# Order of 512-wide and 256-wide products within a weight block, on one core

## Chip, core and metric

The kernel runs on one NeuronCore of a Trainium2 chip. What is compared is the device time of one execution in microseconds (us). It is one program in fp32, with matrix products fed in fp32r (a rounded form of fp32 that TensorE takes in one pass).

## What is computed

Two transformer-like blocks, one after the other, on 256 tokens of width 2048. The first is an RG-LRU mixer with a gated side input, the second a conformer and HGRN mixer followed by a squared-ReLU MLP. Cut to what matters here:

```python
# first block
proj = rmsnorm(x) @ a_w_in                  # stages xb, gate
y = (lru_scan(conv(xb)) * silu(gate)) @ a_w_out          # gates, aout
h = x + rmsnorm(y); h = h + sigmoid(h @ ple_w_gate) * (p @ ple_w_proj)   # pleg, plep
# second block, with modulation vectors from silu(c) @ w_mod
u = modulate(rmsnorm(h)); uc = modulate(rmsnorm(ctx))
i, ff, fb, q, g, cv, cg, gc, gh = split(u @ w_in)        # i, ff, fb also of uc
y_h = readout(hgrn_bidir(q, i, ff, fb, state(uc)), g) @ hgrn_out_w       # hout
y_c = conformer(cv, cg) @ conv_pw_w                      # pw
y = (sigmoid(gc) * y_c + sigmoid(gh) * y_h) @ w_out      # wout
x = h + ga * rmsnorm(y)
out = x + gf * rmsnorm(square(relu(modulate(rmsnorm(x)) @ mlp_w1)) @ mlp_w2)   # mlp1, mlp2
```

All activations stand transposed: features on the 128 partitions, the 256 tokens along the free axis. A tile of a result is 128 features by 256 tokens, summed over the 128-row slices (kt) of its input features.

## The kernel before

**Products in parts.** To keep more bits than fp32r has, both sides are split into a high part and the remainder, the low part. A weight block of 128 x 1024 (eight 128 x 128 weight tiles) lands by DMA in WF (7 buffers); ScalarE (ACT) copies it to WH (the high part, 4 buffers), VectorE (DVE) subtracts to get WL (the low part, 4 buffers). The moving operand lies in SR with its high and low parts side by side, 256 columns each. A full product is WH by high, WH by low and WL by high; low by low is left out.

**Wide and narrow products.** In the stages listed in HALVES (line 54: pleg, cv, cg, q, hout, gh, wout, mlp1, mlp2, pw, gc), one weight tile takes two products: a *wide* one of 512 columns (WH against high and low parts side by side, into the whole PSUM bank) and a *narrow* one of 256 columns (WL against the high part, added to the bank's second half). ACT and DVE add the bank's two halves when the tile is done. The other stages differ: xb, gate, aout, g and a few others use three 256-wide products per weight tile; ff and fb use three 512-wide ones (two token sets at once, read through a strided pattern); i uses three 512-wide ones with the weights as the moving operand. Tile 15 of pleg and of wout (WHOLE, line 55) is done like xb.

**Order.** `timetable()` writes out by hand one list of steps that all engines walk through, each doing its own. A step `prod` is one weight tile (kt) of one result tile. `linear` (line 359) makes one result tile from two weight blocks of eight kt each (h = 0 and 1; for pw and hout from one block), through `product` (line 336), which also calls `tick` after each kt. Every `stride` ticks (4 from the stage cv on, so every four kt), `tick` adds one step of the background work: convolution, states, the HGRN scan (7 levels for each of 4 head pairs, each with a group of TensorE products between ACT and DVE work) and its readout. `linear_quad` (line 370) makes four result tiles at once in four banks, at the start of the stages xb, pleg, cv, i and mlp1, while ACT and DVE are still making the moving operand, two kt per block; its steps `make` do that. Weight blocks are prepared three blocks ahead (LA).

**On TensorE.** The function `product` in `tensor_program` (line 868) turns a step into instructions. It waits on `w_lo` (WL of the block is there, and so WH) at the block's first product, on `free[g]` for the bank at a tile's first one, and on a stage's counter for each kt of its moving operand: `n_lo` (normed input, cv to mlp1), `ys2_lo` (wout), `mid_lo` (mlp2), `ds_lo` (pleg). A wait that was already passed is not issued again. The last product of a block adds to `prod`, which frees WH and WL of that block and tells of finished tiles. For a HALVES stage the two products of a weight tile are ordered by kt: wide then narrow at even kt, narrow then wide at odd kt, so that in a tile made alone pairs of equal width meet.

```python
                for low in ((False, True), (True, False))[kt % 2]:
                    if low:
                        last = mm(cross((kind, j)), wl, hi, False, stop)
                    else:
                        last = mm(bank_of((kind, j))[:, :], wh, flat(moving[kind][:, kt, :, :]), start, stop)
```

Of the kernel before, what the change touches and what calls it, by code (L numbers as in the profile page):

```python
# [74 lines left out]
def timetable():  # L75
# [254 lines left out]
    def tick(n=1):  # L330
        st["since"] += n
        if st["since"] >= st["stride"]:
            st["since"] = 0
            step()

    def product(what, n, first=True, last=True):

        at = len(steps)
        for k in range(n):
            kind, j, h = what  # L340
            off = k * 512 + j % 4 * P if kind == "plep" else (j[2] * 2 + k) * T + j[3] * P if kind == "gates" else k * P
            steps.append(("prod", (kind, j), 8 * h + k, off, first and k == 0, last and k == n - 1, k == n - 1,
                          st["used"], "both"))
            if k + 1 < n:
                tick()
        st["prod"] += 1
        return at

# [21 lines left out]
    def linear_quad(kind, js):  # L370
        for j in js:
            new_tile((kind, j))
        made = 0

        def make(until):
            nonlocal made
            while kind != "i" and made < min(until, KT):
                steps.append(("make", kind, made))
                made += 1

        if kind == "xb":
            make(2)
            prepare(ahead=0)
            low_parts()
        for b in range(8):

            make(2 * b + (4 if kind in ("xb", "pleg") else 2))
            begin(min(LA, b + 1) if kind == "xb" else LA)
            make(2 * b + 4)
            if kind == "xb":  # L390
                if b == 0:
                    steps.append(("load_xr",))
                if b < 6:
                    steps.append(("small", b + 1))
                if b in (5, 6):
                    steps.append(("x_square", b - 5))

            for part in ("high", "low") if kind == "xb" and b == 0 else ("both",):
                for i in range(8):
                    kk, n = divmod(i, 4) if b < 7 else (i % 2, i // 2)  # L400
                    kt = 2 * b + kk
                    steps.append(("prod", (kind, js[n]), kt, 512 * kk if kind == "i" else (4 * kk + n) * P, kt == 0, kt == KT - 1,
                                  part != "high" and (i == 7 or kt == KT - 1), st["used"], part))
                    if kind == "i":
                        tick()
            st["prod"] += 1 if b < 7 else 4
            end()
        if kind == "xb":
            steps.append(("x_scale",))
        for n, j in enumerate(js):  # L410
            evac((kind, j), st["prod"] - 3 + n)
            if chains and chains[-1][:2] == [kind, j]:
                chains[-1][2] = -(n // 2)
            if kind == "mlp1" and n == 1:
                settle()
        advance()
# [172 lines left out]
def build(nc, ctx, ins, out):  # L589
# [158 lines left out]
    def bank_of(what):  # L748
        return bank[tile[what][0]]
# [105 lines left out]
    def tensor_program(tensor):  # L855
        w = Once(tensor)

        def mm(o, l, r, start, stop):
            return tensor.matmul(o, l, r, start=start, stop=stop, skip_group_check=True)  # L859
# [8 lines left out]
        def product(what, kt, off, start, stop, inc, n, part):  # L868
            kind, j = what
            slot = n % NB  # L870
            if kind not in ("gates", "i"):
                hi, lo = moving[kind][:, kt, 0, :], moving[kind][:, kt, 1, :]
            o = psum((kind, j))
            if part == "high":
                w.wait_ge(w_hi, n + 1)
            else:
                w.wait_ge(w_lo, n + 1)
            if start:
                g, uses, _ = tile[(kind, j)]
                w.wait_ge(free[g], uses - 1)  # L880
            if kind in ("xb", "gate"):
                w.wait_ge(n_lo, kt + 1)
            elif kind in ("cv", "cg", "q", "g", "gc", "gh"):
                w.wait_ge(n_lo, 16 + kt + 1)
            elif kind == "i":

                w.wait_ge(n_lo, 32 + kt + 1)
                U, c = (UX, UC)[j % 4 // 2], j % 2 * P
                hi, lo = U[:, kt, 0, c:c + P], U[:, kt, 1, c:c + P]
                wh, wl, o = WH[:, slot, off:off + 512], WL[:, slot, off:off + 512], bank_of((kind, j))[:, :]  # L890
                mm(o, hi, wh, start, False)
                mm(o, hi, wl, False, False)
                last = mm(o, lo, wh, False, stop)
                if inc:
                    last.then_inc(prod, 1)
                return
            elif kind in ("ff", "fb"):
                w.wait_ge(n_lo, 32 + kt + 1)
                o, hi, lo = bank_of((kind, j))[:, :], both(hi), both(lo)
            elif kind == "mlp1":  # L900
                w.wait_ge(n_lo, 48 + kt + 1)
            elif kind == "gates":
                g, b, ri, m = j
                f = 4 * g + 2 * b + kt
                hi, lo = XCs[:, f % 8, 0, :], XCs[:, f % 8, 1, :]
                w.wait_ge(xc_lo, f + 1)
            elif kind == "aout":
                w.wait_ge(ys_lo, kt + 1)
            elif kind == "plep":
                w.wait_ge(ps_lo, kt + 1)  # L910
            elif kind == "pleg":
                w.wait_ge(ds_lo, kt // 2 + 1)
            elif kind == "pw":
                w.wait_ge(cs_lo, kt + 1)
            elif kind == "hout":
                w.wait_ge(oh_lo, kt + 1)
            elif kind == "wout":
                w.wait_ge(ys2_lo, kt + 1)
            elif kind == "mlp2":
                w.wait_ge(mid_lo, 16 * j[0] + kt + 1)  # L920
            wh, wl = WH[:, slot, off:off + P], WL[:, slot, off:off + P]
            if kind in HALVES and what not in WHOLE:

                for low in ((False, True), (True, False))[kt % 2]:
                    if low:
                        last = mm(cross((kind, j)), wl, hi, False, stop)
                    else:
                        last = mm(bank_of((kind, j))[:, :], wh, flat(moving[kind][:, kt, :, :]), start, stop)
            else:
                if part != "low":  # L930
                    mm(o, wh, hi, start, False)
                    mm(o, wh, lo, False, False)
                if part != "high":
                    last = mm(o, wl, hi, False, stop)
            if inc:
                last.then_inc(prod, 1)
# [1314 lines left out]
```

## Time and profile before

| | |
|---|---|
| time, median of 3 runs | 2089.68 us (2088.97 to 2091.5) |
| span of the profiled execution | 2089.8 us |
| TensorE (PE) busy | 2052.2 us, 98% |
| its weight loads (PEld) | 1804.9 us, 86% |
| DVE busy | 1568.9 us, 75% |
| ACT busy | 1035.9 us, 50% |
| DMA, mean | 215 GB/s |

The profile records one execution. The span runs from its first to its last instruction, and lies among the times of the runs. A product's busy time reaches from its start to its modelled end and overlaps the next one's, so the sum of busy times says little of the rate; the distance between starts tells it. The timeline merges equal neighbours on an engine (x2 is two products), and its start is that of the first.

### The profile page before, as it was taken

How to read it: one execution, taken by the hardware profiler on the slowest of the kernel's cores; microseconds unless marked ns; L12 is line 12 of the kernel's file. 1: busy time of each engine (PE TensorE's matmuls, PEld its weight loads, DVE VectorE, ACT ScalarE, POOL GpSimd, SP SyncE). 2: the span in 40 equal slices, each digit the busy share in tenths (PEclk: the TensorE clock that was granted, in tenths of full speed). 3: DMA queues.
4: the chain of work that ended last, by engine and by line, in shares of the span. 5: the costliest groups of instructions: out<-in, count | busy, mean ns of one | idle time of the engine just before them, and what ended most of it. 6: DMA issues, size and time to landing. Idle time of an engine off the chain costs nothing.

```text
span 2089.8 us, 31175 instructions
## 1 busy us (share of the span) xinstructions
PE 2052.2 (98%) x12480; PEld 1804.9 (86%) x12480; DVE 1568.9 (75%) x2370; ACT 1035.9 (50%) x1560; POOL 81.4 (4%) x73
## 2 busy tenths in 40 slices
PE   8999999999999999999999999999999999999997
PEld 8999999888888888998888888788888888888886
DVE  6889986779798686678879898576766756656665
ACT  6876445656423223545555555555445435434543
POOL 0000020110000000000000001200000000000012
PEclk9999999999999999999999999999999999999999
DMA  7778897667524666444438989555875766555552
GB/s 289 233 245 288 299 319 261 235 197 256 162 99 158 206 236 228 140 143 131 141 131 311 336 289 343 164 173 193 275 239 190 258 215 197 181 190 195 188 178 98
DMA packets 122690, 449.87 MB, mean 215 GB/s; under 512 B 13745, under 2 KB 14129, under 8 KB 122033
## 3 DMA queue, kind: packets, MB, share of 16 engines
q1 hardware_dynamic: 122544, 447.88, 63.2%
q8 instruction: 99, 1.62, 0.3%
q14 instruction: 47, 0.38, 0.1%
HBM read 443.63 MB, written 4.19 MB: 214 GB/s over the span
## 4 chain that ended last, share of the span: by engine, by line
PE 72%; DVE 2%; ACT 1%; issue 0%; POOL 0%; POOLq 0%; ACTq 0%; DVEq 0%
PE bank L859 72%; DVE WL L1558 0%; DVE AR L1565 0%; PE bank L1017 0%; DVE SR L1565 0%; ACT WH L1157 0%; DVE AR L1558 0%; ACT AR L1157 0%; ACT AR L1158 0%; ACT L1158 0%; POOL AR L2165 0%; PE bank L1048 0%; ACT SR L1158 0%; POOL AR L2167 0%; DVE AR L1661 0%
## 5 line engine op out<-in xcount | busy, mean ns | idle before, releaser
L859 PE MATMUL bank<-SR,WH 128*128 128x512 f32 (+1 forms) x6240 | 1715.1, 361 | 15.9 <-DVE WL L1558 7.6
L859 PE MATMUL bank<-SR,WL 128*128 128x256 f32 (+1 forms) x4960 | 1124.7, 285 | 1.6 <-DVE SR L1565 1.6
L859 PEld LDWEIGHTS bank<-SR,WL 128*128 128x128 f32 x4960 | 936.8, 189 | 168.5 <-DVE SR L1565 3.0
L859 PEld LDWEIGHTS bank<-SR,WH 128*128 128x128 f32 x6240 | 986.5, 190 | 64.6 <-issue 18.4
L1157 ACT ACTIVATE WH<-WF 128x1024 fp32r<-128x1024 f32 x636 | 671.5, 1057 | 483.7 <-PE bank L859 431.0
L1558 DVE TENSOR_TENSOR WL<-WF,WH 128x1024 fp32r<-128x1024 f32 x636 | 770.2, 1223 | 127.0 <-ACT WH L1157 123.1
L1157 ACT ACTIVATE AR<-bank 128x256 f32<-128x256 f32 (+1 forms) x262 | 107.1, 413 | 312.8 <-PE bank L859 309.5
L1565 DVE SCALAR_TENSOR_TENSOR AR<-WF,SM,AR 128x512 f32<-128x512 f32 (+1 forms) x210 | 208.2, 1017 | 4.6 <-DMA WF<-in_mod 0.2
L1558 DVE TENSOR_TENSOR AR<-AR 128x256 f32<-128x256 f32 (+3 forms) x366 | 149.3, 438 | 48.7 <-ACT AR L1158 33.2
L1558 DVE TENSOR_TENSOR AR<-bank,AR 128x256 f32<-128x256 f32 (+1 forms) x234 | 100.3, 431 | 99.0 <-ACT AR L1157 68.9
L2160 POOL TENSOR_TENSOR AR<-AR 128x256 f32<-128x256 f32 x56 | 68.1, 1216 | 1990.8 <-ACT AR L1158 1990.7
L1558 DVE TENSOR_TENSOR AR<-AR,bank 128x256 f32<-128x256 f32 (+1 forms) x120 | 52.6, 439 | 119.9 <-PE bank L859 91.9
L1158 ACT ACTIVATE AR<-AR 128x256 f32<-128x256 f32 (+2 forms) x165 | 77.3, 474 | 57.9 <-DVE AR L1558 42.8
L1565 DVE SCALAR_TENSOR_TENSOR AR<-AR,PR 128x255 f32<-128x255 f32 (+21 forms) x200 | 89.1, 448 | 6.0
L1157 ACT ACTIVATE SR<-AR 128x256 fp32r<-128x256 f32 (+1 forms) x138 | 58.1, 429 | 47.6 <-DVE AR L1558 33.9
L859 PE MATMUL bank<-WH,SR 128*128 128x512 f32 x256 | 78.9, 389 | 0.0
L1158 ACT ACTIVATE AR<-bank 128x256 f32<-128x256 f32 x58 | 20.5, 382 | 102.2 <-PE bank L859 102.2
L859 PE MATMUL bank<-AR 128*128 128x128 f32 (+1 forms) x416 | 64.1, 297 | 4.6 <-issue 2.8
L859 PEld LDWEIGHTS bank<-AR 128*128 128x128 f32 x416 | 58.4, 191 | 9.0 <-ACT AR L1157 2.9
L1558 DVE TENSOR_TENSOR SR<-AR,SR 128x256 fp32r<-128x256 f32 (+1 forms) x138 | 58.8, 434 | 8.5 <-ACT SR L1157 8.1
L859 PEld LDWEIGHTS bank<-WH,SR 128*128 128x128 f32 x256 | 48.1, 188 | 9.9
L859 PE MATMUL bank<-WL,SR 128*128 128x512 f32 x128 | 49.8, 389 | 0.0
(90 smaller groups left out, 546.6 us busy)
## 6 DMA issues: line engine op xcount, KB each, us to landing
WF<-in_mlp SPq DMA_DIRECT2D x256, 512.0 KB, 4.0
WF<-in_mod SPq DMA_DIRECT2D x192, 512.0 KB, 5.1
WF<-in_w_in SPq DMA_DIRECT2D x176, 512.0 KB, 4.3
WF<-in_a_in SPq DMA_DIRECT2D x64, 512.0 KB, 5.2
WF<-in_a_out SPq DMA_DIRECT2D x32, 512.0 KB, 6.1
WF<-in_ple_g SPq DMA_DIRECT2D x32, 512.0 KB, 4.6
WF<-in_w_out SPq DMA_DIRECT2D x32, 512.0 KB, 5.9
WF<-in_pw SPq DMA_DIRECT2D x16, 512.0 KB, 3.4
```

The costliest lines, as they stand in the source:

```text
L859: return tensor.matmul(o, l, r, start=start, stop=stop, skip_group_check=True)
L1157: return scalar.activation(o, x, f, scale=scale)
L1158: return scalar.activation(o, x, f, scale=scale, bias=bias)
L1558: return vector.tensor_tensor(o, a, b, op)
L1565: return vector.scalar_tensor_tensor(o, a, s, b, op1, op2)
L2160: pool.tensor_tensor(ACC, ACC, SQ[ft % 2], ALU.add).then_inc(acc, 1)
```

## The change

In a HALVES stage a block's eight wide products now stand in one run and its eight narrow ones in another. In a tile made alone the first block (h = 0) has the wide run first, the second block (h = 1) the narrow run first. In tiles made four at a time each block has the wide run first, over both kt and all four tiles; in the last block each tile has its two wide products, then its two narrow ones. A tick follows every second product, so that there are as many ticks in a block as before. The step names the part, and TensorE waits for `w_hi` (WH of the block is there) before wide products and for `w_lo` before narrow ones.

```diff
@@ product
+        kind, j, h = what
+        if kind in HALVES and (kind, j) not in WHOLE:
+            runs = [(part, k) for part in (("high", "low"), ("low", "high"))[h] for k in range(n)]
+            for m, (part, k) in enumerate(runs):
+                steps.append(("prod", (kind, j), 8 * h + k, k * P, first and m == 0, last and m == 2 * n - 1, m == 2 * n - 1,
+                              st["used"], part))
+                if m % 2 and m + 1 < 2 * n:
+                    tick()
...
@@ linear_quad
-            for part in ("high", "low") if kind == "xb" and b == 0 else ("both",):
-                for i in range(8):
-                    kk, n = divmod(i, 4) if b < 7 else (i % 2, i // 2)
...
+            if b == 7 and kind in HALVES:
+                runs = [(part, kk, n) for n in range(4) for part in ("high", "low") for kk in range(2)]
+            elif kind in HALVES or (kind == "xb" and b == 0):
+                runs = [(part, kk, n) for part in ("high", "low") for kk in range(2) for n in range(4)]
+            elif b == 7:
+                runs = [("both", kk, n) for n in range(4) for kk in range(2)]
+            else:
+                runs = [("both", kk, n) for kk in range(2) for n in range(4)]
+            for m, (part, kk, n) in enumerate(runs):
+                kt = 2 * b + kk
...
@@ tensor_program, product
-                for low in ((False, True), (True, False))[kt % 2]:
-                    if low:
-                        last = mm(cross((kind, j)), wl, hi, False, stop)
-                    else:
-                        last = mm(bank_of((kind, j))[:, :], wh, flat(moving[kind][:, kt, :, :]), start, stop)
+                if part == "low":
+                    last = mm(cross((kind, j)), wl, hi, False, stop)
+                else:
+                    last = mm(bank_of((kind, j))[:, :], wh, flat(moving[kind][:, kt, :, :]), start, stop)
```

On TensorE, the second weight block of the first tile of wout (kt 8 to 15) began like this before (kt 8, 9 and half of 10; the rest follows the same pattern):

```order
L859 MATMUL bank<-SR,WH 128x512 [waits ys2_lo,w_lo]
L859 MATMUL bank<-SR,WL 128x256
L859 MATMUL bank<-SR,WL 128x256 [waits ys2_lo]
L859 MATMUL bank<-SR,WH 128x512
L859 MATMUL bank<-SR,WH 128x512 [waits ys2_lo]
```

The same tile's two blocks stand like this now (the first four rows are the first block, kt 0 to 7):

```order
L874 MATMUL bank<-SR,WH 128x512 [waits ys2_lo,free0,w_hi]
L874 MATMUL bank<-SR,WH 128x512 [waits ys2_lo] x7
L874 MATMUL bank<-SR,WL 128x256 [waits w_lo]
L874 MATMUL bank<-SR,WL 128x256 x7
L874 MATMUL bank<-SR,WL 128x256 [waits ys2_lo,w_lo]
L874 MATMUL bank<-SR,WL 128x256 [waits ys2_lo] x7
L874 MATMUL bank<-SR,WH 128x512 [waits w_hi]
L874 MATMUL bank<-SR,WH 128x512 x7
```

The waits for the moving operand have moved to the front of each block, and there is a wait for each of the two weight parts.

On TensorE, the second block of the four cv tiles (kt 2 and 3) before:

```order
L859 MATMUL bank2<-SR,WH 128x512 [waits n_lo,w_lo]
L859 MATMUL bank2<-SR,WL 128x256
L859 MATMUL bank3<-SR,WH 128x512
L859 MATMUL bank3<-SR,WL 128x256
L859 MATMUL bank0<-SR,WH 128x512
L859 MATMUL bank0<-SR,WL 128x256
L859 MATMUL bank1<-SR,WH 128x512
L859 MATMUL bank1<-SR,WL 128x256
L859 MATMUL bank2<-SR,WL 128x256 [waits n_lo]
L859 MATMUL bank2<-SR,WH 128x512
```

and now:

```order
L874 MATMUL bank2<-SR,WH 128x512 [waits n_lo,w_hi]
L874 MATMUL bank3<-SR,WH 128x512
L874 MATMUL bank0<-SR,WH 128x512
L874 MATMUL bank1<-SR,WH 128x512
L874 MATMUL bank2<-SR,WH 128x512 [waits n_lo]
L874 MATMUL bank3<-SR,WH 128x512
L874 MATMUL bank0<-SR,WH 128x512
L874 MATMUL bank1<-SR,WH 128x512
L874 MATMUL bank2<-SR,WL 128x256 [waits w_lo]
L874 MATMUL bank3<-SR,WL 128x256
```

The wait for the second kt has four wide products before it instead of four wide and four narrow ones.

## Rows read from the trace of the kernel before

**Rows 1.** The page: busy time, slices of the span, chain that ended last.

```profile
PE 2052.2 (98%) x12480; PEld 1804.9 (86%) x12480; DVE 1568.9 (75%) x2370; ACT 1035.9 (50%) x1560; POOL 81.4 (4%) x73
...
PEclk9999999999999999999999999999999999999999
...
PE 72%; DVE 2%; ACT 1%; issue 0%; POOL 0%; POOLq 0%; ACTq 0%; DVEq 0%
```

**Rows 2.** Groups by form: busy us, mean ns | idle before, releasers.

```profile
L859 PE MATMUL bank<-SR,WH 128*128 128x512 f32 x4192 | 1339.2, 397 | 8.8 <-DVE SR L1565 3.8 <-DVE WL L1558 3.3 <-DVE SR L1558 1.7
L859 PE MATMUL bank<-SR,WL 128*128 128x256 f32 x4704 | 1025.0, 280 | 1.6 <-DVE SR L1565 1.6
...
L859 PEld LDWEIGHTS bank<-SR,WL 128*128 128x128 f32 x4960 | 936.8, 189 | 168.5 <-DVE SR L1565 3.0 <-issue 1.0
...
L859 PE MATMUL bank<-WH,SR 128*128 128x512 f32 x256 | 78.9, 389 | 0.0
```

**Rows 3.** Timeline, PE, mlp2 into mlp1: start us, length us, instruction, count.

```profile
1699.88 0.62 PE L859 MATMUL bank<-SR,WH 128*128 128x512 f32 x2
1700.34 0.40 PE L859 MATMUL bank<-SR,WL 128*128 128x256 f32 x2
...
1722.87 0.40 PE L859 MATMUL bank<-SR,WH 128*128 128x512 f32 x1
```

**Rows 4.** Timeline, PE, stage ff: 512-wide products alone, first and last.

```profile
689.86 0.61 PE L859 MATMUL bank<-SR,WH 128*128 128x512 f32 x2
...
702.78 0.61 PE L859 MATMUL bank<-SR,WH 128*128 128x512 f32 x2
```

**Rows 5.** Timeline, PE, stage gate: 256-wide products alone.

```profile
189.95 0.40 PE L859 MATMUL bank<-SR,WH 128*128 128x256 f32 x2
190.19 0.28 PE L859 MATMUL bank<-SR,WL 128*128 128x256 f32 x1
...
193.91 0.40 PE L859 MATMUL bank<-SR,WH 128*128 128x256 f32 x2
```

**Rows 6.** Timeline, PE, pleg's four tiles: block boundaries (second product begins the block).

```profile
366.17 0.63 PE L859 MATMUL bank<-SR,WH 128*128 128x512 f32 x2
...
368.96 0.62 PE L859 MATMUL bank<-SR,WH 128*128 128x512 f32 x2
...
371.77 0.63 PE L859 MATMUL bank<-SR,WH 128*128 128x512 f32 x2
```

**Rows 7.** Timeline, wout's first tile: end of its first block, last gated tile.

```profile
1251.22 0.63 PE L859 MATMUL bank<-SR,WH 128*128 128x512 f32 x2
...
1252.70 0.42 DVE L1558 TENSOR_TENSOR SR<-AR,SR 128x256 fp32r<-128x256 f32 x1 [0.48 <-ACT SR L1157]
```

**Rows 8.** Timeline, PE, cv's four tiles: waits for the moving operand.

```profile
461.44 0.28 PE L859 MATMUL bank<-SR,WL 128*128 128x256 f32 x1
...
462.96 0.39 PE L859 MATMUL bank<-SR,WL 128*128 128x256 f32 x1 [1.24 <-DVE SR L1565]
...
477.71 0.38 PE L859 MATMUL bank<-SR,WL 128*128 128x256 f32 x1 [0.18 <-DVE SR L1565]
```

**Rows 9.** Timeline, mlp2's first tile: last piece of MID, first block's end.

```profile
1452.25 0.42 DVE L1558 TENSOR_TENSOR SR<-AR,SR 128x256 fp32r<-128x256 f32 x1 [0.48 <-ACT SR L1157]
...
1452.81 0.63 PE L859 MATMUL bank<-SR,WH 128*128 128x512 f32 x2
```

**Rows 10.** Timeline, cg: waits for WL, and DVE's idle time.

```profile
506.24 0.40 PE L859 MATMUL bank<-SR,WH 128*128 128x512 f32 x1
...
507.48 0.50 PE L859 MATMUL bank<-SR,WH 128*128 128x512 f32 x1 [0.85 <-DVE WL L1558]
...
527.68 0.89 DVE L1565 SCALAR_TENSOR_TENSOR SR<-AR,MODC,SR 128x256 fp32r<-128x256 f32 x2 [1.21 <-ACT SR L1158]
...
530.42 0.50 PE L859 MATMUL bank<-SR,WH 128*128 128x512 f32 x1 [1.95 <-DVE WL L1558]
```

**Rows 11.** Timeline, one level of the scan: ACT's input, TensorE's products.

```profile
956.30 0.72 ACT L1157 ACTIVATE AR<-AR 128x256 f32<-128x256 f32 x2
...
959.95 1.05 PE L859 MATMUL bank<-AR 128*128 128x128 f32 x8
```

More of the change, by code:

```diff
@@ L338, in product @@
         at = len(steps)
[L339 to L345, printed above, removed]
+        kind, j, h = what
[7 more added lines that the diff above has]
+        else:
+            for k in range(n):
+                off = k * 512 + j % 4 * P if kind == "plep" else (j[2] * 2 + k) * T + j[3] * P if kind == "gates" else k * P
+                steps.append(("prod", (kind, j), 8 * h + k, off, first and k == 0, last and k == n - 1, k == n - 1,
+                              st["used"], "both"))
+                if k + 1 < n:
+                    tick()
         st["prod"] += 1
@@ L396, in linear_quad @@
                     steps.append(("x_square", b - 5))
-            for part in ("high", "low") if kind == "xb" and b == 0 else ("both",):
-                for i in range(8):
-                    kk, n = divmod(i, 4) if b < 7 else (i % 2, i // 2)
[L401 to L405, printed above, removed]
+            if b == 7 and kind in HALVES:
[8 more added lines that the diff above has]
+                kt = 2 * b + kk
+                done = part != "high" and kk == 1 and (n == 3 or b == 7)
+                steps.append(("prod", (kind, js[n]), kt, 512 * kk if kind == "i" else (4 * kk + n) * P, kt == 0, kt == KT - 1,
+                              done, st["used"], part))
+                if kind == "i":
+                    tick()
             st["prod"] += 1 if b < 7 else 4
@@ L922, in product @@
             if kind in HALVES and what not in WHOLE:
-                for low in ((False, True), (True, False))[kt % 2]:
-                    if low:
-                        last = mm(cross((kind, j)), wl, hi, False, stop)
-                    else:
-                        last = mm(bank_of((kind, j))[:, :], wh, flat(moving[kind][:, kt, :, :]), start, stop)
+                if part == "low":
+                    last = mm(cross((kind, j)), wl, hi, False, stop)
+                else:
+                    last = mm(bank_of((kind, j))[:, :], wh, flat(moving[kind][:, kt, :, :]), start, stop)
             else:
```

## Prediction

> **What bounds the kernel now.** I read the page from the top: busy shares, slices, chain, then the groups. TensorE is busy 98% of the span, at full granted clock in every slice but for rounding, and the chain that ended last runs through its one matmul line for 72% of the span [rows 1]. So what counts is how closely products follow one another on TensorE, and the few places where it waits. Of its products 4192 are 512 wide with a WH weight, and 4704 are 256 wide with a WL weight; the weight load that each needs takes 189 or 190 ns and lies beside the product before [rows 2]. Of the wide ones 3680 belong to the changed stages: 460 blocks of eight wide and eight narrow products (404 in tiles of two blocks, 32 in tiles of one, 24 in tiles made four at a time), and nothing in the change alters any of these numbers. The busy time of a product overlaps its neighbours', so I go by start to start.
>
> I measured three rhythms in the timeline where nothing else runs on TensorE. **Mixed, as now:** from 1699.88 to 1722.87 stand 132 products, half of each width, so a block of sixteen takes 16 x 22.99 / 132 = 2.787 us [rows 3]. **All 512 wide** (the forget-gate stages): 57 products in 12.92 us, 226.7 ns each [rows 4]. **All 256 wide** (the gate stage of the first mixer): 33 in 3.96 us, 120.0 ns each [rows 5]. Eight of each in unmixed runs would take 1.814 + 0.960 = 2.774 us, 13 ns under the mixed block. Mixing costs something, and the change has one width change in a block where there were eight (two in tiles of one block, since there each block starts with its wide ones).
>
> **The change part by part.**
> Nothing is added or removed but waits. On ACT, DVE, POOL and SyncE the instructions and their order are the same; only TensorE's move. It gets a second wait in each changed block (WH first, WL where the narrow run starts). Bounds for a wait already met: from below 0 (the mixed stretch has a wait at each block start and keeps its 2.787 us throughout [rows 3]), from above the 0.10 us by which the first product after a long wait is longer than its like (0.50 against 0.40 [rows 10]). The second is a restart after idling, not a wait already met, and rows 3 hold eight met ones without a trace of them; I take 0 and leave the upper end out.
>
> *Width changes.* If the 13 ns are spread over eight changes, one costs 1.6 ns. Tiles of two blocks save 7 x 1.6 = 11.4 ns a block, x 404 = 4.6 us; tiles of one save 9.8 x 32 = 0.3 us. The four-at-a-time tiles alternate wide and narrow: two clean blocks take 2.79 and 2.81 us [rows 6]; at 2.777 they would save some 25 ns, x 21 blocks = 0.5 us (their last block of each stage keeps four changes or so, and I give it nothing). Together 5.4 us. Bounds: nothing from below (the mixed cost stays with each product), from above 53 ns a block, if narrow products kept the 115 ns that a pair of them takes now (0.70 us for four products less 0.46 or 0.47 for the wide pair leaves 0.23 [rows 3]) and wide ones fell to 226.7.
>
> *Waits for the moving operand come earlier.* A block used to ask for its last tile of the moving operand at about 2.4 us, now at 1.6 us (wide first) or 0.84 us (narrow first). Three places are short.
> - First tile of the wout stage: its second block starts at 1251.45 and will ask for the last gated tile at 1252.29, but DVE finishes that at 1253.12 [rows 7]: a new stall of 0.8 us.
> - Second block of the cv four: TensorE already waits for the fourth modulated tile until 462.96 [rows 8]. After it came eight products in 1.4 us; now four wide and eight narrow remain, 1.87 us: 0.5 us lost.
> - Last block of the same four: it waits 0.18 us for the last tile until 477.71 [rows 8]; one wide product now stands behind that wait where a narrow one stood in front of it, 0.1 us lost, and the same again in the mlp1 four.
> First tiles of mlp2 are covered: the last piece of MID is ready at 1452.67, and the narrow run, starting at 1453.04, asks for it at 1453.88 [rows 9]; the three other quarters look the same. Without that 1.2 us of cover each would cost what is missing.
>
> *The wait for WL comes later where a block starts wide.* In cg, TensorE stands from 506.47 to 507.48 for a WL [rows 10]. That block starts a tile, its WH is long there, and the narrow run will ask for WL only at 508.3: 1.0 us gained, and 0.7 us in the same way at 513.4. But the 2.1 us stall that ends at 530.42 [rows 10] stands before a second block, which will start with its narrow products and still needs WL, so TensorE, come there earlier, waits longer unless DVE is earlier too. Between 0 and 1.7 us I take 1.0: DVE stood idle for 1.21 us behind ACT at 527.7 [rows 10], so it has that much to give.
>
> *Background work.* Its TensorE pieces still come after every eighth product, but now at the end of a run: mid-block pieces move by +0.47 us (wide first) or -0.47 us (narrow first), those at block ends stay. A mid-block piece at 959.95 had its last input from ACT at 957.02, 2.9 us before [rows 11], so I book 0. Without that cover, 28 levels of the scan would each cost up to 0.47 us.
>
> Sum: 2089.8 - 5.4 + 0.8 + 0.5 + 0.2 - 1.0 = 2084.9 us. The profiled span is 2089.8 us and the median of the runs 2089.68, so no correction is due: **2084.9 us, 0.23% faster**. What a measurement of this kernel can tell from no change is about 0.2%, or 4.2 us.
>
> **A rule against the numbers above.** Uniform runs here show 226.7 and 120.0 ns, or N / 2.4 plus 13 ns for either width [rows 4, 5]. The Trainium skill (TensorE: Matmul & The Clock Gate, Back-to-back issue gap) gives N / 2.4 + 2.5 ns, 216 and 109 ns, for products with no load between them; by it a block would take 2.60 us and the kernel some 80 us less. The trace disagrees wherever a load precedes each product.
>
> **The rivals.**
> 1. *The cost is not in the mixing.* Wide products of these stages cost what they cost (233 ns, 0.46 to 0.47 us for two [rows 3]), and so do narrow ones (115 to 118). For it: a block of the four-at-a-time tiles with some fourteen changes takes 2.79 us [rows 6], hardly more than 2.787 with eight. Against it: the sum of the unmixed rhythms, and the means of 389 and 397 ns of unmixed and mostly mixed wide products [rows 2]. Then a block stays within 3 ns, and only the waits act: +0.5 us, 2090. Chance 0.26.
> 2. *Slower: runs of narrow products lose their cover.* Each product's weights load while the one before streams. Now a narrow product stands next to a wide one, and the pair of narrow ones takes 0.23 us; in a long run each takes 120 ns [rows 5]. If the wide ones do not fall from 233 to 226.7 at the same time (the stages of [rows 4] read a strided moving operand, these a flat one), a block takes 8 x 233 + 8 x 120 = 2.824 us, +37 ns x 428 = +16 us: 2106. It decides once wide products in a run stay above 2.787 / 8 - 0.120 = 228.4 ns. Against it: the stage that makes i moves WH, flat and 512 wide, and its products have the mean of 389 ns that the strided ones have, where the mixed ones have 397 [rows 2]. Chance 0.10. The Trainium skill (same page, LDWEIGHTS) puts a load of 128 columns at 107 ns, as long as 256 columns stream, which leaves a narrow run no slack; the rows' 120 ns would hold that price already.
> 3. *Much faster:* wide at 226.7 and narrow at 115: 53 ns x 428 = 23 us, 2066. Against it stand the 120.0 of [rows 5], without one exception. Chance 0.04.
> 4. *The waits eat it:* background pieces that come 0.47 us early meet unready inputs, DVE falls behind, and half of the places named cost double: about +4 us on the forecast, 2089. Chance 0.08.
>
> **How the numbers follow.** The forecast (mixing costs 1.6 ns a change, the waits as named) has 0.52; its own spread of 2081 to 2088 lies across the 0.2% line at 2085.5, and I give 0.42 of it to the faster side, 0.10 to no change. With 0.04 of rival 3 and a little of 4, faster has 0.47; no change has 0.26 + 0.10 + some of 4, 0.40; slower has rival 2 and a tail of waits, 0.13. The range 2079 to 2093 leaves out rivals 2 and 3.
>
> **What would show it.** In the profile after, a wide run in mlp1 or mlp2 should show starts 226 to 227 ns apart and a narrow run 120; a block 2.775 us from start to start. Wide runs at 233 with narrow at 120 mean rival 2, both at today's values rival 1. At the start of wout TensorE should idle 0.8 us behind DVE's subtraction, the fourth tile of cv should cost half a microsecond more, and the WL stalls at the start of cg should be gone. The forecast is wrong if a block saves under 5 ns or over 20, or if TensorE's idle time in the scan grows by more than 2 us.

## The result and the profile after

The changed kernel takes 2093.08 us (median of 20 runs, 2088.69 to 2096.2), the one before 2090.88 us (20 runs beside them, 2086.28 to 2091.65). The ratio is 1.0015, with an interval of 1.0008 to 1.0021: 1.7 to 4.4 us slower, within the 0.2% that I called no change, and on the other side of it than forecast. The forecast was 2084.9 us with a range of 2079 to 2093; the median lies just above its end. The profiled executions have spans of 2091.5 us (after) and 2089.8 us (before).

The page after, with the same three places as [rows 1]:

```profile
PE 2052.5 (98%) x12480; PEld 1818.7 (87%) x12480; DVE 1569.3 (75%) x2370; ACT 1035.3 (49%) x1560; POOL 84.3 (4%) x73
...
PEclk9999999999999999999999999999999999999998
...
PE 71%; DVE 3%; ACT 1%; issue 0%; POOL 0%; POOLq 0%; ACTq 0%; DVEq 0%
```

The same picture: TensorE is busy all the time. Busy time did not move by more than 0.3 us, although the order of some 7400 products did. The groups by form, which answer to the first two of [rows 2] (busy us, mean ns of one | idle before, releasers), hold both halves of the answer:

```profile
L874 PE MATMUL bank<-SR,WH 128*128 128x512 f32 x4192 | 1051.9, 392 | 8.8 <-DVE SR L1579 6.9 <-DVE SR L1572 1.7
...
L874 PE MATMUL bank<-SR,WL 128*128 128x256 f32 x4704 | 781.6, 284 | 4.4 <-DVE WL L1572 3.6 <-DVE SR L1572 0.8
```

A wide product's mean fell from 397 to 392 ns and a narrow one's rose from 280 to 284: five off 4192 and four on 4704 nearly cancel. The idle time in front of the narrow ones rose from 1.6 to 4.4 us, that in front of the wide ones stayed at 8.8. These are the waits that the change moved.

The waits, and at the end the rhythm in the stretch that [rows 3] show, in the timeline (start us, length us, instruction, count, idle time before it and its releaser):

```profile
461.12 1.09 PE L874 MATMUL bank<-SR,WH 128*128 128x512 f32 x4
...
463.91 0.50 PE L874 MATMUL bank<-SR,WH 128*128 128x512 f32 x1 [1.70 <-DVE SR L1579]
...
470.11 1.19 PE L874 MATMUL bank<-SR,WH 128*128 128x512 f32 x4 [0.32 <-DVE SR L1579]
...
476.31 0.96 PE L874 MATMUL bank<-SR,WH 128*128 128x512 f32 x3 [0.32 <-DVE SR L1579]
...
512.87 0.86 PE L874 MATMUL bank<-SR,WL 128*128 128x256 f32 x5 [1.14 <-DVE WL L1572]
...
519.19 0.50 PE L874 MATMUL bank<-SR,WL 128*128 128x256 f32 x2 [0.50 <-DVE WL L1572]
...
532.76 0.62 PE L874 MATMUL bank<-SR,WL 128*128 128x256 f32 x3 [1.99 <-DVE WL L1572]
...
848.28 0.66 PE L1062 MATMUL bank<-CN,AR 128*128 128x128 f32 x4 [0.36 <-DVE AR L1572]
...
1255.03 0.43 DVE L1572 TENSOR_TENSOR SR<-AR,SR 128x256 fp32r<-128x256 f32 x1 [0.48 <-ACT SR L1171]
1255.51 0.38 PE L874 MATMUL bank<-SR,WL 128*128 128x256 f32 x1 [0.75 <-DVE SR L1572]
...
1701.70 3.82 PE L874 MATMUL bank<-SR,WH 128*128 128x512 f32 x16
1705.36 2.08 PE L874 MATMUL bank<-SR,WL 128*128 128x256 f32 x16
1707.27 3.82 PE L874 MATMUL bank<-SR,WH 128*128 128x512 f32 x16
```

The last three rows: runs meet back to back between tiles (second block narrow then wide, next tile wide first), so they are sixteen long, and a tile takes 1707.27 - 1701.70 = 5.57 us; over all the tiles after 1605 us a block takes 2.783 us. The forecast was 2.775. The rows above them are the waits of the four cv tiles (461 to 476), of cg (512 to 532), of q (848) and of wout's first tile (1255); I come back to each.

By stages, from the end of one stage's last product to the end of the next one's (us):

```
        before  after   change   what I had forecast for it
cv       55.59  56.97    +1.38   +0.6 of waits, less rhythm
cg       49.14  49.11    -0.03   -1.0 and rhythm
q        53.13  53.66    +0.53   rhythm alone
pw       62.60  62.25    -0.35   rhythm
wout     89.80  90.28    +0.48   +0.8 and rhythm
pleg, gc, gh, hout, last quarter of mlp2, together:  -0.27
xb      133.95 135.49    its instructions are untouched
mlp1    647.27 646.18    -1.09; without its first block (below) +0.7
```

mlp1's row holds the first three quarters of mlp2 too. Adding the changed stages, with +0.7 for mlp1, gives +2.4 us; the runs say +3.1 (1.7 to 4.4). xb moved without a change, and mlp1's first block, counted from wout's end, took 23.9 us before and 22.2 after. Both hold stretches of 3.4 us in which the granted clock reads half, 1.2 of 2.4 GHz. Before shows them at 38.4, 1345.7 and 1359.4 us, after at 39.6 and 1360.6 with one of 6.8 us at 12.3. Ahead of the two in mlp1 TensorE had idled 1.9 us (until 1345.3) and 3.0 us (until 1358.2), ahead of the one at 38.4 twice about 1 us. mlp1's first block takes 20.85 us in profiles that have neither stretch (runs of four, pairs with cg wide first), 22.1 to 22.6 in those with one and 23.9 to 24.1 in those with both, so one is worth 1.2 to 1.9 us, and which of them an execution has differs from one to the next. So single spans of this kernel can't be compared below 2 us; stages can, though not to the last tenth: aout, which has no changed instruction, takes 99.32 us in this profile of before and 98.77 to 98.79 in all the others.

The mean granted clock that each run records gives a second comparison, with before as it ran beside the experiments below. At 0.995 before averages 2089.9 us (37 runs) and after 2092.3 (10 runs), +2.4. At 0.994, 0.996 and 0.997 the change costs 2.9, 1.0 and 2.9 us (5, 3 and 5 runs of after). The mean over these 23 runs is +2.4 us, as by stages.

### The profile page after: what moved, and what is told of

Same layout as the page of the kernel before. It is cut to its first block, busy times and chain, and to the rows that moved or that the text cites. A ratio compares the mean times of both kernels' runs of the same rounds, so it can differ in the third digit from the quotient of the medians.

```text
span 2091.5 us, 31176 instructions
## 1 busy us (share of the span) xinstructions
PE 2052.5 (98%) x12480; PEld 1818.7 (87%) x12480; DVE 1569.3 (75%) x2370; ACT 1035.3 (49%) x1560; POOL 84.3 (4%) x73
## 4 chain that ended last, share of the span: by engine, by line
PE 71%; DVE 3%; ACT 1%; issue 0%; POOL 0%; POOLq 0%; ACTq 0%; DVEq 0%
PE bank L874 70%; DVE WL L1572 1%; DVE AR L1572 1%; DVE AR L1579 0%; DVE SR L1579 0%; ACT WH L1171 0%; PE bank L1031 0%; ACT AR L1171 0%; DVE AR L1989 0%; ACT SR L1172 0%; ACT AR L1172 0%; DVE SR L1572 0%; PE bank L1062 0%; POOL AR L2179 0%; DVE AR L1575 0%
## 5 line engine op out<-in xcount | busy, mean ns | idle before, releaser
L874 PE MATMUL bank<-SR,WH 128*128 128x512 f32 (+1 forms) x6240 | 1429.9, 358 | 14.9 <-DVE SR L1579 6.9
L874 PEld LDWEIGHTS bank<-SR,WH 128*128 128x128 f32 x6240 | 1090.4, 190 | 185.8 <-issue 18.6
L874 PE MATMUL bank<-SR,WL 128*128 128x256 f32 (+1 forms) x4960 | 881.3, 290 | 4.4 <-DVE WL L1572 3.6
L874 PEld LDWEIGHTS bank<-SR,WL 128*128 128x128 f32 x4960 | 723.5, 191 | 36.8 <-DVE WL L1572 4.4
```

## The experiments

Two theories stood after this. **A, later products behind a wait:** the runs help a little in tiles made alone, and the four-at-a-time tiles lose more than that, at waits that I had missed. **B, added waits:** the second wait in each changed block costs something, some 7 ns, wherever it stands. The experiments came in three groups, each on one chip together with before, whose medians were 2089.9, 2090.3 and 2089.47 us. Most have 11 runs; runs of four have 6, of one 2, of three 8.

### Which part costs: tiles made alone, or tiles made four at a time

Linear only: the four-at-a-time tiles in their old order, the rest as changed. Quads only: the reverse. Pairs with two waits: the old order everywhere, with the new waits for WH and WL. Quads only has the two waits in its tiles made alone as well (its expectation below says a single one); it differs from pairs with two waits in the four-at-a-time tiles alone.

```diff
# linear only, and pairs with two waits: linear_quad
-            if b == 7 and kind in HALVES:
...
+            if kind in HALVES:
+                order = [(kk, n) for n in range(4) for kk in range(2)] if b == 7 else [(kk, n) for kk in range(2) for n in range(4)]
+                runs = [(part, kk, n) for kk, n in order for part in (("high", "low"), ("low", "high"))[kk]]
...
# quads only, and pairs with two waits: product
-            runs = [(part, k) for part in (("high", "low"), ("low", "high"))[h] for k in range(n)]
+            runs = [(part, k) for k in range(n) for part in (("high", "low"), ("low", "high"))[k % 2]]
```

> Only tiles made alone get the runs; tiles made four at a time keep the old order. Theory A (in the changed profile a two-block tile takes 5.566 us against 5.574 before, and what was lost was lost in the four-at-a-time starts of pleg, cv and mlp1, where the wait for the second kt of a block comes after four wide products): tiles made alone give back 202 x 7.5 ns = 1.5 us, the start of wout costs 0.9 us, so about 0.5 us faster than before, ratio 0.9998, and cv from its first block to its last takes 22 us as before instead of 23.2. Theory B (the second wait in each block costs, 436 blocks): as slow as the whole change, about +2 to +3 us.

> Only the tiles made four at a time get the runs (24 blocks); tiles made alone keep the old order and their single wait before both parts. Theory A: +1.5 to +2.5 us on the kernel before, with stalls of 0.4 to 1.9 us at the second kt of cv's blocks 1, 3, 5 and 7. Theory B (the waits of 436 blocks): within 0.5 us of before.

> The old order of products everywhere, but each product waits for its own part (WH or WL) as in the changed kernel, so a block has two such waits. Theory A: nothing, 2.787 us a block, time within 1 us of before. Theory B (a met wait costs some 7 ns): 2.794 us a block and +3 us.

Measured: linear only 2089.46 us, 0.9998 (0.999 to 1.0007); quads only 2093.18, 1.0015 (1.0006 to 1.0024); pairs with two waits 2089.63, 0.9999 (0.999 to 1.0008).

The 460 added waits cost nothing that can be seen: in pairs with two waits no changed stage is over 0.01 us longer than before (mlp1 from its second block on), and cg and wout are 0.2 us shorter (in cg the first stall for WL is 0.62 us instead of 0.85, since a wide product no longer waits for it). The four-at-a-time tiles alone hold the whole loss: quads only is 3.3 us above before, more than the 1.5 to 2.5 expected, and linear only is level with it. The row 463.91 above is the wait for the fourth normed tile. It ends 5.7 us after the stage's first product, as it did before, but only four wide products stand before it in its block now, and four wide and eight narrow ones behind it; and the blocks at 470.11 and 476.31 stand for 0.32 us where the blocks before the change had none. Each of these three blocks takes 0.45 to 0.5 us more. The waits of TensorE (us in total, times, longest) show the same of before

```profile
PE bank L859 <- DVE WL L1558: 7.6, 6, 2.8
PE bank L859 <- DVE SR L1565: 5.4, 5, 3.0
```

and of quads only:

```profile
PE bank L874 <- DVE SR L1579: 7.6, 9, 3.0
```

Four stalls and 2.2 us more for one kind of releaser. cv takes 57.02 us here against 55.59, and mlp1's first tiles, from their second block on, 22.34 us after against 20.97 before: +1.4 us each. In the third such stage, pleg, no wait within the first four tiles is longer than 0.04 us, and they take 23.51 us after against 23.48 before.

### What a width change costs: the length of the runs

The waits explain the quads, but not why the runs bring so little: some 7 ns a tile in the rhythm. So I changed the length of the runs, in tiles made alone, with the four-at-a-time tiles in the old order (but for wide first).

```diff
# wide first in every block (runs of 8)
-            runs = [(part, k) for part in (("high", "low"), ("low", "high"))[h] for k in range(n)]
+            runs = [(part, k) for part in ("high", "low") for k in range(n)]
# runs of four
+            runs = [(part, k + r) for r in range(0, n, 4) for part in ("high", "low") for k in range(4)]
# runs of one
+            runs = [(part, k) for k in range(n) for part in ("high", "low")]
# runs of three
+            runs = [(part, k) for lo, hi in ((0, 3), (3, 6), (6, 8)) for part in ("high", "low") for k in range(lo, hi)]
...
```

> The changed kernel, but every block starts with its wide run, also the second of a tile, so a tile has two changes from narrow to wide instead of one. Theory A1 (a change from narrow to wide costs about 27 ns in the five wide products after it and gives 8 ns back in the next narrow ones, whether 8 or 16 narrow products stood before it): 2.793 us a block, 5.586 us a tile, 4 us slower than the changed kernel less the 0.9 us that wout's first tile no longer waits: +5 to +6 us on before. Theory A2 (the cost grows with the number of narrow products before the change, as a backlog that they build up): 13 ns for 8 of them, tile 5.566 us, time as the changed kernel or 1 us under it.

> Tiles made alone: four wide, four narrow, four wide, four narrow in each block; tiles made four at a time in the old order. Measures what one change from narrow to wide costs after four narrow products. Seen so far: 3.3 ns net a change with pairs (2.787 us a block, four changes), 19.4 ns net after 8 or 16 narrow ones. Theory S (the price is full as soon as enough wide ones follow to pay it: the five wide products after the change are 6, 9, 1, 6 and 4 ns longer, four of them fit in here): 14 ns net, block 2.802 us, +6 us on before. Theory D (the price is for the number of narrow products before the change, growing up to 8 of them): about 8 ns, block 2.789 us, +1 us.

> Tiles made alone: wide and narrow alternate through the whole block, eight changes from narrow to wide in a block. If every change had its own price of 3.3 ns or more, 2.800 us or longer a block and at least +5 us on before. If the price shrinks with the run (one wide product after a narrow one cannot be charged 27 ns), the block stays between 2.774 and 2.787 us and the time between 5 us less and the same as before.

> Tiles made alone: runs of three, three and two in each block, three changes from narrow to wide. One change costs 7 ns with runs of one, 3.4 with two, 17 with four, 19 with eight. If the price rises smoothly from two to four, about 10 ns with three: 2.798 us a block. If four is where it jumps, 2.785; if three is already as dear as four, 2.812.

Measured: wide first 2093.03 us, 1.0014 (1.0005 to 1.0023); runs of four 2094.95, 1.0025 (1.0013 to 1.0037); runs of one 2102.11, 1.0061 (1.0043 to 1.0079); runs of three 2092.64, 1.0007 (0.9996 to 1.0017). Wide first was expected at +5 to +6 us and came at +3.1: its blocks take the 2.793 us expected, but cg, q and wout give back 1.8, 0.5 and 0.5 us against the changed kernel, of which the expectation had counted wout alone. Their timelines, each from the start of a run to the start of the like one. Wide first:

```profile
1701.65 2.00 PE L874 MATMUL bank<-SR,WH 128*128 128x512 f32 x8
1703.49 1.11 PE L874 MATMUL bank<-SR,WL 128*128 128x256 f32 x8
1704.45 2.00 PE L874 MATMUL bank<-SR,WH 128*128 128x512 f32 x8
```

Runs of four, over eight blocks:

```profile
1700.70 1.09 PE L875 MATMUL bank<-SR,WH 128*128 128x512 f32 x4
...
1723.15 1.09 PE L875 MATMUL bank<-SR,WH 128*128 128x512 f32 x4
```

Runs of one, over 59 pairs of a wide and a narrow product, 353 ns a pair:

```profile
1700.08 0.40 PE L875 MATMUL bank<-SR,WH 128*128 128x512 f32 x1
...
1720.93 0.40 PE L875 MATMUL bank<-SR,WH 128*128 128x512 f32 x1
```

Runs of three, three and two, over eight blocks:

```profile
1701.71 0.63 PE L875 MATMUL bank<-SR,WH 128*128 128x512 f32 x2
...
1724.08 0.63 PE L875 MATMUL bank<-SR,WH 128*128 128x512 f32 x2
```

The mean distance from a product's start to the next start, by its place in its run, taken over all such products of mlp1 and mlp2 after 1605 us (84 to 1357 for a place; at some places one distance, over 45 ns longer than the rest, is left out), tells what happens. Unmixed it is 226.7 ns for a wide and 120.0 ns for a narrow product [rows 4, 5].

```
runs of     wide, 1st 2nd 3rd ...           narrow, 1st 2nd ...       over     under    per narrow-to-
                                                                      226.7    120.0    wide change
1           236.5                           116.8                      9.8     -3.2      6.6 ns
2 (before)  232.9 233.4                     114.6 115.8               12.9     -9.6      3.3 ns
3, 3, 2     234.0 234.2 227.5               114.9 117.8 119.6         15.6     -7.8      7.8 ns
4           234.2 234.6 232.1 228.3         117.5 119.6 118.7 118.3   22.3     -5.9     16.4 ns
8           233.3 235.8 228.3 232.5 230.8   113.4 119.2, then 120.0   27.2     -7.5     19.7 ns
            then 226.7
16 (after)  233.3 235.8 228.3 232.5 230.8   113.3 119.2, then 120.0   27.0     -7.5     19.5 ns
            then 226.7
```

("Over" is the sum, over the places of a run, of what its products take above 226.7 ns, "under" the same below 120.0.) So the surcharge is not paid per width change, nor is it a property of mixed products. After narrow products the first **five** wide ones are 1.6 to 9.1 ns late, 27 ns in all, whether eight or sixteen narrow ones came before; after wide ones the first two narrow products are early, 7 or 8 ns. The place counts and not the kt: in the changed kernel the ninth to the sixteenth wide product are kt 0 to 7 of the next tile and take 226.7 ns, and the same kt come late in wide first. Runs of four pay most of the surcharge twice a block. Pairs never reach the third wide product and have the largest rebate, 9.6 ns on two narrow ones. By blocks, in us: runs of one 2.827, pairs 2.787, threes 2.797, fours 2.807, eights 2.793, and the change, with one narrow-to-wide change a tile, 2.783 us. The rhythm of pairs was already within 4 ns of the best that I found, and 13 ns above the 2.774 us of unmixed products; the change takes off 3 to 4 ns of these 13.

### The waits: can they be had the other way round

Quads by kt: tiles made alone as changed; the four-at-a-time tiles in runs of four banks, one kt after the other, so that a kt of the operand is asked for as late as before. Fitted: the same, with pairs in wout's first tile and wide first in both blocks of cg. Pairs with cg wide first: the old order everywhere except cg. Fitted with q: as fitted, q wide first in both blocks too.

```diff
# quads by kt, fitted, fitted with q: linear_quad
...
+            if kind in HALVES and b == 7:
+                runs = [(part, kk, n) for n in range(4) for kk in range(2) for part in (("high", "low"), ("low", "high"))[kk]]
+            elif kind in HALVES:
+                runs = [(part, kk, n) for kk in range(2) for part in (("high", "low"), ("low", "high"))[kk] for n in range(4)]
...
# fitted: product (with q: kind not in ("cg", "q"))
-            runs = [(part, k) for part in (("high", "low"), ("low", "high"))[h] for k in range(n)]
+            if (kind, j) == ("wout", 0):
+                runs = [(part, k) for k in range(n) for part in (("high", "low"), ("low", "high"))[k % 2]]
+            else:
+                runs = [(part, k) for part in (("high", "low"), ("low", "high"))[h if kind != "cg" else 0] for k in range(n)]
# pairs, cg wide first: product
+            if kind == "cg":
+                runs = [(part, k) for part in ("high", "low") for k in range(n)]
+            else:
+                runs = [(part, k) for k in range(n) for part in (("high", "low"), ("low", "high"))[k % 2]]
```

> The changed kernel, but in tiles made four at a time the runs stay within one kt: four wide, four narrow of the first kt, then four narrow, four wide of the second (in the last block the old order). The wait for the second kt stands again after eight products. Theory A (what the change lost, it lost there): cv's start takes 31.6 us instead of 33.0, mlp1's start loses its 1.4 us too, and the time is within 0.1% of before, about 2.5 to 3 us under the changed kernel. Rival (the long runs over four banks were not the cause): as the changed kernel, +3 us.

> The kernel of the run before, and besides: wout's first tile in the old order of pairs, and the cg stage with the wide run first in both blocks of a tile. If the 0.9 us stall at the start of wout and the WL stalls of cg are what is left of the losses, about 2.5 us faster than before: 1.6 us from the runs, 1.4 us from cg (its eight tiles pay 0.16 us for a second change), ratio 0.9988. Rival: DVE, late in cg, gives the gain back in the next stage, and the ratio is 0.9995.

> The order of before everywhere, except in cg, where each block has its wide run first. Asks how much of the fitted kernel's 3.6 us comes without any runs elsewhere. By stages: cg gains 1.5 to 1.8 us, the rest nothing: ratio 0.9992 to 0.9994, and the fitted kernel stays ahead by the 1.6 us of its runs. Rival: the runs are worth nothing at all outside cg, and this kernel is as fast as the fitted one.

> The fitted kernel, and in the q stage the wide run first in both blocks too. The q stage took 53.65 us with the narrow run first in second blocks, and 53.12 with the wide run first in all: 0.5 us faster there, ratio to before 0.9980. Rival: the wait in q only moves to the next stage, and the ratio stays 0.9983.

> The changed kernel as it stands, on the same chip as the two above: ratio 1.0012 to 1.0015, as in its first measurement, so that the fitted one lies 5 to 7 us under it.

Measured: quads by kt 2090.3 us, 1.0001 (0.9992 to 1.001); fitted 2086.31, 0.9983 (0.9975 to 0.9992); pairs with cg wide first 2086.14, 0.9983 (0.9974 to 0.9992); fitted with q 2086.41, 0.9984 (0.9975 to 0.9992); the changed kernel again 2090.47, 1.0012 (1.0003 to 1.0021). Four expectations were missed: fitted came 1 us under its 0.9988, pairs with cg wide first 2 us under its 0.9992 to 0.9994 and level with fitted (the rival that it names); the changed kernel again is 4 us above the fitted ones and not 5 to 7; and fitted with q did not come under fitted, though its stage q did get 0.5 us shorter and the next stage, g, no longer.

```
stage       before  after  quads by kt  fitted  pairs, cg wide  fitted with q  wide first
cv           55.59  56.97     55.54      55.49      55.54          55.52         57.04
cg           49.14  49.11     49.11      47.35      47.36          47.35         47.33
q            53.13  53.66     53.65      53.65      53.13          53.10         53.12
wout         89.80  90.28     90.28      89.26      89.58          89.26         89.76
```

*cv.* In quads by kt the fourth tile's wait is what [rows 8] show for before, 1.24 us with four narrow and four wide products behind it, and the stage is back at 55.54 us:

```profile
461.39 0.74 PE L876 MATMUL bank<-SR,WL 128*128 128x256 f32 x4 [1.24 <-DVE SR L1581]
```

So the quad's loss is the order of its waits, not its runs.

*cg.* Wide first in both blocks takes 1.75 us off against the changed kernel, whatever stands around it. In the change the first tile's wait for WL is gone from its start as forecast (506.47 in [rows 10]), but TensorE then comes to the second block, narrow first, a moment after its start, and stands 1.14 us for that WL (512.87 in the timeline after), 0.50 at 519.19 and still 1.99 at 532.76. Here the order with cg wide first, everything else in pairs:

```profile
525.23 2.14 PE L878 MATMUL bank<-SR,WH 128*128 128x512 f32 x8 [0.67 <-ACT WH L1175]
...
528.35 1.22 PE L878 MATMUL bank<-SR,WL 128*128 128x256 f32 x8 [0.98 <-DVE WL L1576]
```

and fitted, the same pair of waits at the same place:

```profile
526.55 2.10 PE L879 MATMUL bank<-SR,WH 128*128 128x512 f32 x8 [0.67 <-ACT WH L1176]
...
529.67 1.21 PE L879 MATMUL bank<-SR,WL 128*128 128x256 f32 x8 [1.02 <-DVE WL L1577]
```

The 1.95 us in front of a block in [rows 10] has become 0.67 for WH and 0.98 for WL, with 2.1 us of wide products between them that used to wait for both. This stall is no cheaper for it: the block that begins at 525.23 and the one ahead of it take 7.80 us together, and 7.79 before the change. The gain lies at the two earlier stalls for WL, 0.85 us at 507.48 [rows 10] and 0.54 us at 514.13 before, 1.14 and 0.50 us in the changed kernel; with wide first 0.09 us is left of them. Here DVE, which makes WL and also the modulated operand, is what TensorE runs into, so what matters is that WL is asked for last.

*q and wout.* After q's narrow run at 845.85 TensorE comes to a background piece at 848.28, whose last input from DVE is 0.36 us late. Before the change this piece started at 846.00 without a stall. With q wide first the stage takes 53.10 us again. wout gives back 1.0 us when its first tile alone keeps its pairs.

*pw.* Its gain of 0.35 us comes with the runs (62.23 to 62.27 us in every kernel that has long runs there, 62.58 to 62.65 in the others), and it too is a background piece. Before and after:

```profile
949.72 1.13 PE L859 MATMUL bank<-AR 128*128 128x128 f32 x8 [1.71 <-issue]
...
952.53 1.13 PE L874 MATMUL bank<-AR 128*128 128x128 f32 x8 [1.26 <-issue]
```

Both start 14.33 us after the stage's first product. The piece comes half-way through a block, behind eight wide products now and not four of each width, so TensorE comes to it later and waits 0.45 us less; "issue" says that the profile shows no releaser. The runs' rhythm in tiles of one block takes 0.1 us of that back.

*What can't be told apart.* Fitted is 0.9983 and pairs with cg wide first is 0.9983. The stages put fitted some 1.2 us ahead (the rhythm of its runs, pw and wout, less q), inside the interval of 1.8 us to either side. Against runs of before at equal mean clock fitted is 3.1 us faster and pairs with cg wide first 2.8 (means over 11 runs each), which leans the same way and settles no more. Of the latter's gain the stages of its profile show 2.0 us (cg 1.8, wout 0.2); where the rest comes from is open. The plain reading of the whole case is that the gain over before, 0.17% of the time (0.08 to 0.25%), can be had, as far as the times tell, by one stage's order of waits without any run elsewhere.

The changed kernel again shows what one profile is worth. Its windows (us; then each engine's busy us and count, granted clock, DMA share, GB/s) over cg's last tiles, against the same window of the first execution:

```profile
530.00:550.00 20.00, 18.52 (x97) 16.10 (x98) 13.69 (x18) 9.68 (x16) 0.00 (x0) 0.91 0.66 211
```

in the repeated run, and in the first one:

```profile
530.00:550.00 20.00, 18.01 (x107) 15.86 (x106) 15.07 (x21) 11.14 (x18) 0.00 (x0) 1.00 0.65 213
```

Ten products fewer in 20 us, at a mean granted clock of 0.91: a half-clock stretch of 3.4 us at 532.8, after a stall of 1.98 us for WL that ends at 531.5, and cg at 50.71 instead of 49.11 us. The program is the same.

## Why the prediction was wrong

Its sum was 2089.8 - 5.4 + 0.8 + 0.5 + 0.2 - 1.0. Term by term:

1. **Width changes, -5.4 us: this step failed.** "If the 13 ns are spread over eight changes, one costs 1.6 ns." The unmixed rhythms were right to a tenth: 226.7 ns from the sixth wide product on, 120.0 from the third narrow one. So was the direction. But the cost of a change depends on the length of the runs beside it: 3.3 ns per narrow-to-wide change for pairs, 19.5 for long runs. Of eight narrow-to-wide changes in a tile one was left, and it costs six times as much. Measured: 7 ns a tile, 3.4 ns a block, x 404 = -1.4 us; in tiles of one block, by the 2.793 us of wide first against 2.787, +0.2 us. That is -1.2 where the first term's share was -4.9: 3.7 us are missing here, the largest miss of all terms. A block saved under 5 ns, which the prediction had named as a sign of being wrong.
2. **The waits of the four-at-a-time tiles, +0.5 and +0.2 with the quads' own gain of 0.5 in the first term: mis-sized.** Measured +1.4 in cv and +1.4 in mlp1, 2.8 us in all. The fourth tile's half microsecond was there. What I missed is that two tiles of operand are made per block all through these stages and TensorE is hardly behind ACT and DVE in any of them: I looked only for waits that the trace of before showed, and cv's fourth and sixth block, which had none there but little slack, got 0.5 us each. mlp1, which I booked at 0.1, has the same pattern: 0.34 us each in its third, fifth and seventh block and 0.4 us in the others together. The wait at 477.71 [rows 8], which I called the last block's, is the seventh's (kt 13); in cv that block lost nothing.
3. **cg, -1.0 us: nothing, by the mechanism that I gave as its lower bound.** The stall at the tile's start went, and came back in the next block, which asks for WL first. DVE's idle time of 1.21 us [rows 10] was not TensorE's to have. Quoted as 0 to 1.7, I took the middle; 0 was right, and the 1.7 are what wide first in both blocks brought.
4. **wout, +0.8 us: right.** 0.75 us behind DVE's subtraction, at the row predicted; the stage's net +0.5.
5. **The first tiles of mlp2 and the added waits, 0: right, or 0.2 us better each in cg and wout.** The pairs with two waits show the second.
6. **Background work, 0: right in sum.** One place lost 0.36 us, in q, and one gained 0.45 us, in pw, where TensorE used to wait for the piece. The rival that gave it +4 us was far too large, though its mechanism, an early piece at an unready input, is the one seen.

By the measured sizes the sum is 2089.8 - 1.2 + 2.8 + 0.8 + 0.4 - 0.4 + 0 = 2092.2, +2.4 us, within the interval of both measurements (1.7 to 4.4, 0.6 to 4.4). Of the rivals (whose prices are multiplied by 428 blocks where 436 stand in tiles made alone, which changes none of them by more than 0.5 us), the first (the mixing costs nothing, 2090) came nearest in time; as a mechanism it was wrong, since the wide products did fall to 226.7. The second had half of a truth: wide products after a narrow run stay near 233, as it says, but only the first five. Its test, the mean of a run above 228.4 ns, is met by runs of eight (1.84 us between starts, 230 ns) and gives wide first its 2.793 us.

Not settled: why the surcharge reaches over five products, and why pairs have the largest rebate. It goes with the width and not with the weight buffer, as far as rows tell: ff uses WH and WL in turn at one width and runs at 226.7 throughout [rows 4], the gate stage the same at 120.0 [rows 5]. Whether the operand read, the PSUM write or the weight load carries it was not tried.

## What to carry to other kernels

A cost per switch must be measured at two run lengths before it is multiplied by the number of switches; here grouping eight times longer saved 3 to 4 ns of 13, and three or four in a run were worse than two. When products of a block are reordered, list for each block which input it asks for last and put there what the slowest producer makes, and look at blocks that show no wait as well: their slack is what the new order spends. Where differences are a few microseconds of two thousand, compare stages between fixed points and leave out the stretches of half clock, or compare runs of equal mean clock.

## What was unexpected

- The first five wide products after a long narrow run take 233, 236, 228, 233 and 231 ns instead of 226.7, the same after eight and after sixteen narrow ones; the first two narrow ones after a long wide run take 113 and 119 instead of 120.0.
- The block's time is not monotonic in the length of its runs: 2.827, 2.787, 2.797, 2.807, 2.793 and 2.783 us for 1, 2, 3, 4, 8 and 16.
- The same program drops to half clock for 3.4 us after some of its idle stretches and not after others. In the first 6.00 us from mlp1's first product on, before (from 1358.15) has 26 products at a mean granted clock of 0.72, and pairs with cg wide first (from 1352.37), with the same order of products there, 34 at 1.00; both had idled 3.0 us until then. The first block of that stage, counted from wout's end, took 23.9 and 20.85 us.
